# Weight sums of three block products per quarter by an accumulating DMA, in place of a vector subtraction one quad earlier

## The reference

```python
u = rmsnorm(h, norm_ff_pre[l])
f = jnp.square(jax.nn.relu(u @ w_ff1[l])) @ w_ff2[l]     # (256 x 2048) @ (2048 x 8192), then @ (8192 x 2048)
h = h + rmsnorm(f, norm_ff_post[l])
```

## Time and profile before

| | us |
|---|---|
| median of 3 runs | 1320.65 |
| profiled execution, its own time | 1320.38 |
| its span, first to last instruction | 1318.6 |
| PE busy | 1307.8 |
| DVE busy | 923.9 |
| ACT busy | 668.3 |
| POOL busy | 47.0 |

### The profile page before, as it was taken

One profiled execution on the slowest core, in us unless ns is written; L12 is line 12 of the kernel. 1 busy time (PEld: TensorE's weight loads), 2 busy tenths in 40 slices (PEclk: granted clock), 3 DMA queues, 4 the chain that ended last, 5 costly groups with the idle time before them and its releaser, 6 DMA issues.

```text
span 1318.6 us, 18299 instructions
## 1 busy us (share of the span) xinstructions
PE 1307.8 (99%) x6998; PEld 1118.0 (85%) x6998; DVE 923.9 (70%) x1265; ACT 668.3 (51%) x922; POOL 47.0 (4%) x92
## 2 busy tenths in 40 slices
PE   9999999999999999999999999999999999999998
PEld 8889989888888888888988888887888878888886
DVE  7765565687875555547868866589876899676554
ACT  7554454465664444454645665445454464445442
POOL 1222110000000000000000000000000000000000
PEclk9999999999999999999999999999999999999999
DMA  9766555555566666774774656746477464776663
GB/s 301 220 182 170 164 161 163 156 166 159 169 191 191 189 192 205 229 244 154 239 255 161 236 185 189 236 151 213 151 222 238 142 208 160 234 251 188 225 194 105
DMA packets 135498, 256.75 MB, mean 195 GB/s; under 512 B 8308, under 2 KB 45584, under 8 KB 134781
## 3 DMA queue, kind: packets, MB, share of 16 engines
q1 hardware_dynamic: 131360, 243.50, 58.4%
q0 software_dynamic: 2160, 4.74, 1.7%
q10 hardware_dynamic: 1900, 7.46, 1.6%
HBM read 251.39 MB, written 4.27 MB: 194 GB/s over the span
## 4 chain that ended last, share of the span: by engine, by line
PE 93%; DVE 3%; DMA 2%; issue 0%; ACT 0%; SPq 0%; ACTq 0%
PE bank L2041 17%; PE bank L1731 11%; PE bank L1733 11%; PE bank L1732 11%; PE bank L2044 9%; PE bank L2091 5%; PE bank L2092 5%; PE bank L2093 5%; PE bank L1777 4%; PE bank L1765 3%; PE bank L1766 3%; PE bank L1764 3%; PE bank L1779 2%; DMA s_raw<-in_w_ff 1%; PE bank L2065 1%; DVE b_lo L1570 1%
## 5 line engine op out<-in xcount | busy, mean ns | idle before, releaser
L1050 DVE TENSOR_TENSOR w_lo<-raw,w_hi 128x1024 fp32r<-128x1024 f32 (+1 forms) x360 | 429.9, 1210 | 248.2 <-ACT w_hi L586 246.8
L586 ACT ACTIVATE w_hi<-raw 128x1024 fp32r<-128x1024 f32 (+1 forms) x360 | 371.2, 1047 | 295.3 <-DMA raw<-in_w_ff 173.2
L2041 PE MATMUL bank<-f_hl,w_hi 128*128 128x512 f32 x960 | 229.7, 391 | 0.0
L2041 PEld LDWEIGHTS bank<-f_hl,w_hi 128*128 128x128 f32 x960 | 176.4, 188 | 34.1
L2044 PEld LDWEIGHTS bank<-f_hl,w_lo 128*128 128x128 f32 x960 | 123.1, 191 | 4.7
L2044 PE MATMUL bank<-f_hl,w_lo 128*128 128x256 f32 x960 | 124.5, 283 | 0.0
L1731 PE MATMUL bank<-w_hi,u_hl 128*128 128x512 f32 x256 | 101.1, 395 | 0.0
L1733 PE MATMUL bank<-w_hi,u_hl 128*128 128x512 f32 x256 | 99.9, 390 | 0.0
L1732 PE MATMUL bank<-w_lo,u_hl 128*128 128x512 f32 x256 | 99.8, 390 | 0.0
L906 ACT ACTIVATE s_hi<-s_raw 128x1024 fp32r<-128x1024 f32 x48 | 50.7, 1055 | 75.3 <-DMA s_raw<-in_w_ff 75.3
L1765 PE MATMUL bank<-u_hl,w_lo 128*128 128x272 f32 x288 | 82.4, 289 | 0.0
(11 more groups left out here) (282 smaller groups left out, 2311.1 us busy)
## 6 DMA issues: line engine op xcount, KB each, us to landing
raw<-in_w_ff SPq DMA_DIRECT2D x160, 512.0 KB, 4.1
raw<-in_w_in SPq DMA_DIRECT2D x128, 512.0 KB, 3.7
s_raw<-in_w_ff SPq DMA_DIRECT2D x48, 512.0 KB, 3.9
b_raw<-in_w_ff SPq DMA_DIRECT2D x24, 1024.0 KB, 5.2
raw<-in_w_out SPq DMA_DIRECT2D x32, 512.0 KB, 4.5
raw<-in_w_branch_b SPq DMA_DIRECT2D x16, 512.0 KB, 3.8
raw<-in_w_branch_a SPq DMA_DIRECT2D x16, 512.0 KB, 3.8
xt<-in_turned_x SPq DMA_DIRECT2D x8, 272.0 KB, 5.6
```

The lines of the kernel that those rows point to most:

```text
L586: act.activation(w_hi[:, u, :, 0:width], raw[:, u, :, 0:width], ACT.Copy).then_inc(hi_ready, 1)
L1050: dve.tensor_tensor(w_lo[:, u, :, 0:width], raw[:, u, :, 0:width], w_hi[:, u, :, 0:width].bitcast(F32), ALU.subtract).then_inc(lo_ready, 1)
L2041: ins = pe.matmul(acc[g][:], w_hi[:, u, k, cols], f_hl[:, kt, :], start=kt == 0, stop=kt == KT - 1)
```

## The change

For W3, W4 and W5 of each of the first three quarters (`BY_DMA`), the two sums that `sum` made are made by DMA:

- SP issues, right behind the quad's load, a second load of 256 KB, of the quad's fourth tile into weight slot 4 (`b_copied`).
- POOL waits for both loads and then issues a DMA from slots 1 and 2 of the quad into slots 3 and 4 that adds to what stands there (512 KB, from SBUF to SBUF, `b_added`).
- DVE has no `sum` for these three: it waits for `b_added` in front of `sum2`. `sum2` and `sum4` stand in the quad's own step, on both sides of its first S, and not one quad ahead. The sums of W6 and W7 are where they were.
- ACT's order is unchanged, but its `rest` of these quads now waits for a `sum4` of the same step.
- Signs: the scheme's sums are now additions (an accumulating DMA adds), which turns two signs in the hidden rows' sums and two in the final join. The number and the sizes of these instructions are the same.

The diff, cut to its core:

```diff
+BY_DMA = (3,4,5)
 for _k in range(2, N_W):
     HI_ORDER += [("first", _k), ("S", 2 * _k - 1), ("rest", _k), ("S", 2 * _k)]
-    if _k < 6:
-        _n = SUM_ORDER[_k + 1]
-        LO_ORDER += [("S", 2 * _k - 1), ("sum", _n), ("first", _k), ("sum2", _n), ("rest", _k), ("sum4", _n), ("S", 2 * _k)]
...
+    LO_ORDER += [("sum", _k), ("sum2", _k)] if _k in BY_DMA else []
+    LO_ORDER += [("S", 2 * _k - 1)]
+    LO_ORDER += [("sum4", _k)] if _k in BY_DMA else []
...
+                if k in BY_DMA:
+                    sp.dma_start(b_raw[i][:, 4, :], w_ff2[0, bass.ds(q * D + (4 * j + 1) * P, P), slice(c * 1024 + CW, c * 1024 + 1024)])\
+                      .then_inc(b_copied[i], 16)
...
+            for q in range(QUARTERS - 1):
+                for k in BY_DMA:
+                    i = B_SLOT[k]
+                    pool.wait_ge(b_landed[i], b_lands(q, k, 16))
+                    pool.wait_ge(b_copied[i], b_sums(q, k))
+                    pool.dma_start(b_raw[i][:, 3:5, :], b_raw[i][:, 1:3, :], accum_op=ALU.add).then_inc(b_added[i], 16)
...
-                if kind == "sum":
+                if kind == "sum" and n in BY_DMA:
+                    dve.wait_ge(b_added[i], b_sums(q, n))
+                    dve.sem_inc(b_part, 1)
+                elif kind == "sum":
                     dve.wait_ge(b_landed[i], b_lands(q, n, 16))
-                    dve.tensor_tensor(raw_b[:, 4:2:-1, :], raw_b[:, 3:0:-2, :], raw_b[:, 2:4, :], ALU.subtract)\
+                    dve.tensor_tensor(raw_b[:, 4:2:-1, :], raw_b[:, 3:0:-2, :], raw_b[:, 2:4, :], ALU.add)\
                        .then_inc(b_part, 1)
```

More of the change, by code:

```diff
@@ L103 @@
     HI_ORDER += [("first", _k), ("S", 2 * _k - 1), ("rest", _k), ("S", 2 * _k)]
-    if _k < 6:
-        _n = SUM_ORDER[_k + 1]
-        LO_ORDER += [("S", 2 * _k - 1), ("sum", _n), ("first", _k), ("sum2", _n), ("rest", _k), ("sum4", _n), ("S", 2 * _k)]
[L107 to L110, removed]
+    LO_ORDER += [("sum", _k), ("sum2", _k)] if _k in BY_DMA else []
+    LO_ORDER += [("S", 2 * _k - 1)]
+    LO_ORDER += [("sum4", _k)] if _k in BY_DMA else []
+    LO_ORDER += [("sum", 6), ("sum2", 6), ("sum4", 6)] if _k == 6 else []
+    LO_ORDER += [("sum", 7), ("first", 5), ("sum2", 7), ("rest", 5), ("sum4", 7)] if _k == 5 else [("first", _k), ("rest", _k)]
+    LO_ORDER += [("S", 2 * _k)]
 HI_ORDER += [("S", N_S - 1)]
@@ L332, in hybrid_block @@
         b_landed = [sem(f"b_landed{i}") for i in range(3)]
+        b_copied = [sem(f"b_copied{i}") for i in range(3)]
+        b_added = [sem(f"b_added{i}") for i in range(3)]
         h2_stored, h2_landed = sem("h2_stored"), sem("h2_landed")
@@ L382, in b_lands, with b_sums @@
             return each * (B_BEFORE[n] + 1 + q * B_COUNT[B_SLOT[n]])
+        def b_sums(q, n):
+            mine = [k for k in BY_DMA if B_SLOT[k] == B_SLOT[n]]
+            return 16 * (mine.index(n) + 1 + q * len(mine))
         def hi_no(q, kind, n):
@@ L1514, in activate_hidden @@
                 dve.wait_ge(hid_part, n + 1)
-                dve.tensor_tensor(work[:, 8, :], work[:, 3, :], work[:, 1, :], ALU.add).then_inc(hid_part, 1)
+                dve.tensor_tensor(work[:, 8, :], work[:, 3, :], work[:, 1, :], ALU.subtract).then_inc(hid_part, 1)
                 dve.wait_ge(hid_part, n + 2)
@@ L1519, in activate_hidden @@
                 dve.wait_ge(hid_part, n + 3)
-                dve.tensor_tensor(work[:, 10, :], work[:, 0, :], work[:, 9, :], ALU.subtract).then_inc(hid_ready, 1)
+                dve.tensor_tensor(work[:, 10, :], work[:, 0, :], work[:, 9, :], ALU.add).then_inc(hid_ready, 1)
             def keep_hidden(q, j, last):
@@ L1558, in split_item @@
                     dve.wait_ge(b_part, part + 1)
-                    dve.tensor_tensor(raw_b[:, 5, :], raw_b[:, 1, :], raw_b[:, 4, :], ALU.subtract).then_inc(b_part, 1)
+                    dve.tensor_tensor(raw_b[:, 5, :], raw_b[:, 1, :], raw_b[:, 4, :], ALU.add).then_inc(b_part, 1)
                 elif kind == "sum4":
                     dve.wait_ge(b_part, part + 2)
-                    dve.tensor_tensor(raw_b[:, 6, :], raw_b[:, 0, :], raw_b[:, 5, :], ALU.subtract).then_inc(b_ready, 1)
+                    dve.tensor_tensor(raw_b[:, 6, :], raw_b[:, 0, :], raw_b[:, 5, :], ALU.add).then_inc(b_ready, 1)
                 elif kind == "first":
@@ L1599, in join @@
                                       for b in range(BLOCKS) for h in range(2)]
-                dst, other = ((c11, p1), (p6, p1), (p7, p6), (c21, p7), (p6, p5), (c12, p6), (p7, p5), (c22, p7))[step]
+                dst, one, other = ((c11, c11, p1), (p6, p6, p1), (p7, p7, p6), (c21, c21, p7), (p6, p5, p6), (c12, c12, p6),
+                                   (p7, p5, p7), (c22, c22, p7))[step]
                 if step:
                     dve.wait_ge(p_part, step)
-                ins = dve.tensor_tensor(dst, dst, other, ALU.add).then_inc(p_part, 1)
+                dve.tensor_tensor(dst, one, other, ALU.subtract if step in (4, 6) else ALU.add).then_inc(p_part, 1)
                 if step == 7:
```

## The result

| | before | after |
|---|---|---|
| median of 11 runs | 1321.29 (1320.21 to 1324.07) | 1324.88 (1323.31 to 1326.39) |
| ratio, 95% interval | | 1.0026 (1.0018 to 1.0034) |
| profiled execution, span | 1320.38, 1318.6 | 1324.88, 1323.1 |

What follows compares the result with a forecast made beforehand. PE was taken to bound the kernel, with at most 5.0 us to gain from its waits for DVE. -0.6 + 0.7 = +0.1 us on the profiled 1320.38, the median 0.3 above: 1320.6 us, no change, range 1316.4 to 1327.

Steps and rivals of the forecast that it cites:

- PE alone bounds, and 5.0 us are to be had.: PE is busy 1307.8 of 1318.6 us; its waits for DVE in three second stages cost 5.0 us, the most to gain.
- The chain from S5 to the end of W3's `rest` becomes 6.03 us.: DVE's work from S5's start to the end of W3's `rest` takes 6.03 us where it was 6.84, 0.8 shorter.
- S5 comes 1.2 us later by the second loads.: On SP's queue, W4's second load puts S5 back by 0.65 us and W3's, through S2 and S4, by 0.55.
- The first rival: S5 isn't later: extra loads find gaps or S2's delay doesn't reach S4; 4.6 us gained, 1315.8; chance 0.20.
- -0.6 us for all but the DMAs' share.: PE's stalls at W3 and `add_x`, with S5 later and DVE's chain shorter: +0.4 in q = 0, -0.5 in q = 1 and 2.
- The adding DMA takes 7.2 us and is hidden.: POOL's 512 KB adding DMA lands 7.2 us after issue, within W4's 9.4 us of room before DVE wants the sums.
- The second rival: W4's sum by DMA comes too late, delaying `sum2` and DVE behind it: +4.6 us, 1325.0, or 1335 at 16 us; chance 0.17.
- the two signs by which the forecast was to show itself wrong: S5 landing as before would mean faster; DVE's `sum2` of W4 standing idle for the DMA would mean slower.
- S7 then comes 1.3 to 2.6 us late, +0.35 each in q = 1 and 2, +0.7.: W4's adding DMA takes 1.3 us more of the DMA engines than a 512 KB load, delaying S7; ends 0 and +1.6 each.
- The third rival: The adding DMAs hold back loads of S5, S7 and S9: one us on S5 gives 1323.6, two 1326.6; chance 0.13.

Runs made afterwards that it cites:

- S5 first: S5's load issued ahead of W4's: in the kernel before 1319.50 us, ratio 0.9990; in the changed kernel 1330.81 us, ratio 1.0075.
- the order alone: The changed order against the kernel before, with DVE making the sums itself in the quad's own step, no second loads, no POOL DMA: 1321.41 us, ratio 1.0003.

## Why the prediction was wrong

- *PE alone bounds, and 5.0 us are to be had.* Right: no kernel of these comes below 0.9990. The best profile loses 3.8 us, not 0.
- *The chain from S5 to the end of W3's `rest` becomes 6.03 us.* Right: 905.56 to 911.6 us, with 0.19 idle for ACT. W2's stall went, W3's stayed; 3.9 us of loss where 4.2 were forecast.
- *S5 comes 1.2 us later by the second loads.* Right: it lands 1.2, 0.8 and 1.0 us later than before, counted from the stage's first matmul, and S5 first removes the stall. The first rival is out: even without the adding DMAs the gain is 1.2 us, not 4.6.
- *-0.6 us for all but the DMAs' share.* Within the interval: -1.2 (-2.4 to 0). In part by luck: the profile without the adding DMAs has 2.1 us of loss at S2 and S5, which the sum doesn't have, and none at `add_x`, as forecast.
- *The adding DMA takes 7.2 us and is hidden.* 5.6 us; hidden for itself, with no idle time of DVE for it in any quarter. The second rival isn't what happened here. So neither of the two signs by which the forecast was to show itself wrong (S5 landing as before, DVE idle for the DMA) came up, and it was slower all the same: S7 had no sign of its own.
- ***S7 then comes 1.3 to 2.6 us late, +0.35 each in q = 1 and 2, +0.7.* This is the step that failed.** Its place and its kind were right, its size wasn't: S7 lands 3.8, 3.8 and 2.6 us later than before, counted from the stage's first matmul, and the term is 4.6 us (about 3.0 to 6.2), where its upper end was +3.2. Two things were wrong in it. I took the difference between a load of 1 MB and one of 512 KB, 1.3 us, for what the DMA holds; the traces show 3.1 us of all 16 engines, and 3.6 for W4's. And I took this time as shared. In fact SP's queue stood nearly still for three of it, so W5's 1.25 MB began late, and S7 behind them was later by the DMA's whole time and the slower start. W5's second load, which the prediction left out here, has little part in it: without W4's DMA S7 lands 0 and 0.4 us later than before in q = 1 and 2. Then q = 0 isn't exempt: W4's and W5's `rest` are late there as well, 1.3 us in sum.
- The third rival had the mechanism, share and not lateness, for S5, S7 and S9, with 0.13. Its price was worked out for S5 alone; the runs show it at S7.

The forecast took the change for a small gain and a small loss. The runs show three larger terms, with the order alone at +0.5 us (-0.8 to 1.6): the second loads some +2.9, DVE's nine sums taken away some -4.5, the adding DMAs +4.6, each with about 1.7 us to either side. What stays open: no run leaves out both the sums and the second loads (that they cost the same there is read from W3's loss), and what the instruction packet costs over many executions.

## What to carry to other kernels

A DMA that takes work from a vector engine is paid in the time of the DMA engines: count its reads and its writes, take that time as closed to the loads, and ask which load is issued in it and who waits for that one. Freeing an engine that is 70% busy brings at most PE's waits for it, and here those hung on the landing of loads as well. In a stream of loads that comes just in time, put such a DMA where nothing urgent is issued (W3's and W5's cost nothing that could be measured, W4's nearly all), and expect a load that is moved ahead to make another late.

## What the runs showed of the hardware

- A DMA from SBUF to SBUF of 512 KB with addition took 5.6 us from issue to landing (4.4 to 5.8) and 49 us of engine time in the changed kernel; a plain one 23.5 us of engine time, with addition on half the bytes the same.
- While it ran, loads of another queue didn't share evenly: 122 packets to 7 in three microseconds. Among running loads, by contrast, it took 11.0 us itself (issued at 908.57, with S5 first).
- A load of 512 KB took some 1.2 us longer when a 16 KB packet of instructions, 0.93 us on one engine, fell among its own (S2: 4.8 to 5.5 us in 12 stages, 3.6 to 4.5 in 33). Where the loads come just in time, PE lost 0.8 us with it. That the packet is the cause isn't shown by a run of its own.
- After PE had waited 3.13 us, the kernel with S5 first gave it the lower of the clock's two levels, 1.2 GHz, for a while. By stage (us, busy us of PE, PEld, DVE, ACT, POOL, granted clock, DMA share, GB/s):

```profile
922.50:924.00 1.50, 1.50 (x6) 1.25 (x7) 1.47 (x2) 1.02 (x1) 0.00 (x0) 0.89 1.02 235
924.00:926.70 2.70, 2.70 (x7) 1.74 (x6) 2.51 (x2) 2.70 (x3) 0.00 (x0) 0.50 0.62 200
```

Starts stood 0.43 us apart there in place of 0.23, 1.3 us more on top of the wait. In q = 2 the same followed a wait of 1.97 us (granted clock 0.50 from 1101.3 to 1103.5). After the changed kernel's wait of 1.68 us nothing like it is seen.
